# A projection by seven block products instead of eight, in two passes over halves of the tokens

## The chip, the cores and the metric

One Trainium2 chip, one core. The metric is device time in microseconds (us), the median of several runs of the whole program. The program is one layer of a decoder trunk; the change is in its first stage, the combined input projection.

## The reference

```python
h = rms_norm(x, g_mix[l])            # x: (1, 2048, 1024) float32
proj = h @ w_in[l]                   # w_in: 1024 x 7168
qkv = proj[..., :4608]               # q, k, v of three attention groups, 512 columns each
u = proj[..., 4608:5120]
gate_a, gate_b = proj[..., 5120:6144], proj[..., 6144:]
q = head_rms_norm(qkv[:, :, 0], q_gain[l]) * (HEAD_DIM ** -0.5)
k = head_rms_norm(qkv[:, :, 1], k_gain[l])
...                                  # attention, state space model, their mix, 32 experts
```

So the projection is a product of 2048 x 1024 by 1024 x 7168, with a sigmoid on the gates and a mean of squares over each head of 64 columns for q and k.

## The kernel before

`project` runs first (from 2.5 to 1283 us of the trace). Its 7168 columns are 14 matrices of 512 columns: u, then v, q and k of three groups, then four of gates. Each number is split into a high and a low part (fp32r), and a product is three matmuls: high by high, high by low, low by high.

All the tokens stay in SBUF, turned, as `hh` and `hl` (1024 x 2048 each). They are made in the first matrix, one token tile of 128 ahead: ScalarE squares (L520) and takes the root (L525), VectorE scales (L614), TensorE turns by eight transposes (L443), ScalarE writes the high part (L530) and VectorE the low one (L620).

For each matrix, 8 slices of the weights (128 x 512, `raw`) are loaded by SP's queue (L320) and split by ScalarE (`wh`, L542) and VectorE (`wl`, L625). Then 16 tiles of output follow, each of 8 slices x 3 = 24 matmuls of 128 x 128 by 128 x 512 into one of six PSUM banks (`po`, L493): 14 x 16 x 24 = 5376 matmuls. ScalarE takes u, v and gates out of PSUM (L561). A q or k tile takes five steps on two engines: squares on ScalarE (L551), a sum of each head (L634) and its mean (L637) on VectorE, roots on ScalarE (L553), and on VectorE the reciprocal (L639) and the product out of PSUM (L645). SP's queue stores each tile (L338).

The order on each engine is the order in which the code is written, tile by tile; one engine lets another go by semaphores. GpSimd makes 16 pairs of maps for the state space model beside the gate matrices (L274 to L303), and TensorE and VectorE finish a pair between two tiles (L456, L463, L787 to L794). VectorE computes the powers that these need in one piece (`maps`, beside a q matrix) and the tables in another (`table`).

## Time and profile before

| | |
|---|---|
| median of 3 runs | 4809.84 us (4809.36 to 4812.94) |
| the profiled execution | 4809.9 us, its span 4808.3 us |
| projection, first to last matmul of L493 | 15.9 to 1283 us |
| TensorE busy over the span | 97% |
| VectorE, ScalarE, GpSimd busy | 57%, 40%, 15% |
| granted TensorE clock | 0.987 of full speed (2.4 GHz) |

A matmul's duration in the profile (390 ns) is longer than the distance from one to the next, since they are pipelined: what counts is how many start in a stretch. The busy share of an engine is an average over stages that have different limits. A row of the timeline gives start, duration, engine, line, operation, and in brackets how long the engine had been idle and who ended that.

### The profile page before, as it was taken

What the parts mean: (1) busy time and instruction counts of PE and PEld (TensorE: products, weight loads), DVE (VectorE), ACT (ScalarE), POOL (GpSimd) and SP (SyncE); (2) the same over time, 40 slices, a digit from 0 to 9 for tenths busy, and PEclk for the clock granted to TensorE, in tenths of its full rate; (3) what the DMA queues carried; (4) which work ended last, traced back from release to release, by engine and by line L of the source; (5) the groups of instructions that cost most, each with busy time, mean ns of one, the idle gap of its engine ahead of it and who ended that gap; (6) DMA issues with size and microseconds to landing.
All of it is one profiled execution on the core that took longest, in us unless ns stands there. A gap on an engine that the chain in (4) does not pass through costs nothing.

```text
span 4808.3 us, 75561 instructions
## 1 busy us (share of the span) xinstructions
PE 4674.5 (97%) x26332; PEld 4097.3 (85%) x26332; DVE 2757.7 (57%) x5732; ACT 1916.0 (40%) x3152; POOL 697.2 (15%) x783
## 2 busy tenths in 40 slices
PE   8999999999889999999799999999999999999998
PEld 7888888878679987788699999999988888999997
DVE  4343333111266678555555556666667777778887
ACT  4212112111136673133233334344445555556665
POOL 0000000233202101222101111111111111111121
PEclk9999999999999999999899999999999999999999
DMA  4322222322453445543445555656566667677777
GB/s 136 115 71 77 73 85 81 115 90 91 128 205 136 139 163 184 185 134 136 176 151 176 189 177 190 204 179 215 179 229 215 208 231 241 237 244 268 279 262 254
DMA packets 262082, 823.24 MB, mean 171 GB/s; under 512 B 39273, under 2 KB 70804, under 8 KB 224341
## 3 DMA queue, kind: packets, MB, share of 16 engines
q1 hardware_dynamic: 228728, 715.02, 41.3%
q0 software_dynamic: 28304, 88.03, 7.9%
q10 hardware_dynamic: 4829, 17.31, 1.0%
q8 instruction: 131, 2.15, 0.2%
q14 instruction: 90, 0.74, 0.0%
HBM read 661.67 MB, written 163.88 MB: 172 GB/s over the span
## 4 chain that ended last, share of the span: by engine, by line
PE 51%; DVE 0%; ACT 0%; issue 0%; DVEq 0%; POOL 0%; DMA 0%; ACTq 0%; SPq 0%; POOLq 0%
PE ex_d L2453 14%; PE ex_g L2420 10%; PE ex_g L2422 9%; PE ex_g L2416 7%; PE ex_d L2416 4%; PE ex_d L2447 3%; PE ex_d L2422 2%; PE ex_g L2397 1%; PE ex_d L2397 0%; PE ex_d L2428 0%; DVEq L2224 0%; ACT ex_wgh L2500 0%; DVE ex_x L2615 0%; DVE ex_y L2689 0%; DVE ex_wgl L2597 0%
## 5 line engine op out<-in xcount | busy, mean ns | idle before, releaser
L2422 PE MATMUL ex_g<-ex_x,ex_wgl 128*128 128x256 f32 (+12 forms) x3456 | 980.0, 284 | 0.0
L2420 PE MATMUL ex_g<-ex_x,ex_wgh 128*128 128x288 f32 (+5 forms) x3584 | 756.1, 303 | 1.7 <-DVE ex_x L2615 1.7
L2422 PEld LDWEIGHTS ex_g<-ex_x,ex_wgl 128*128 128x128 f32 x3456 | 652.3, 189 | 4.3
L2597 DVE TENSOR_TENSOR ex_wgl<-ex_wg,ex_wgh 128x2048 fp32r<-128x2048 f32 x274 | 626.8, 2288 | 42.4 <-ACT ex_wgh L2500 42.3
L2500 ACT ACTIVATE ex_wgh<-ex_wg 128x2048 fp32r<-128x2048 f32 x274 | 523.5, 1910 | 280.7 <-PE ex_g L2422 274.0
L2420 PEld LDWEIGHTS ex_g<-ex_x,ex_wgh 128*128 128x128 f32 x3584 | 592.7, 188 | 11.1 <-DVE ex_x L2615 2.0
L2416 PE MATMUL ex_g<-ex_x,ex_wgh 128*128 128x512 f32 (+6 forms) x1664 | 527.5, 375 | 0.9 <-DVE ex_t L2627 0.9
L493 PE MATMUL prj_p<-prj_wh,prj_hh 128*128 128x512 f32 x1280 | 500.9, 391 | 1.4 <-DVE prj_hl L620 1.4
L493 PE MATMUL prj_p<-prj_wh,prj_hl 128*128 128x512 f32 x1280 | 499.0, 390 | 0.0
L493 PE MATMUL prj_p<-prj_wl,prj_hh 128*128 128x512 f32 x1280 | 499.0, 390 | 0.0
L2453 PE MATMUL ex_d<-ex_wdh,ex_ath 128*128 128x512 f32 x992 | 398.4, 402 | 1.1 <-DVE ex_ath L2655 1.1
L2453 PE MATMUL ex_d<-ex_wdh,ex_atl 128*128 128x512 f32 x992 | 391.1, 394 | 0.0
L2453 PE MATMUL ex_d<-ex_wdl,ex_ath 128*128 128x512 f32 x992 | 391.0, 394 | 0.0
L2365 POOL DMA_INDIRECT out<-ex_y,ex_cur x82 | 155.5, 1897 | 1513.4 <-ACT ex_y L2521 1246.6
L2507 ACT ACTIVATE ex_wdh<-ex_wd 128x1024 fp32r<-128x1024 f32 x273 | 287.8, 1054 | 180.1 <-PE ex_d L2447 116.8
L2416 PEld LDWEIGHTS ex_g<-ex_x,ex_wgh 128*128 128x128 f32 x1664 | 312.2, 188 | 42.6 <-issue 1.2
L2603 DVE TENSOR_TENSOR ex_wdl<-ex_wd,ex_wdh 128x1024 fp32r<-128x1024 f32 x272 | 331.8, 1220 | 21.5 <-ACT ex_wdh L2507 20.7
L493 PEld LDWEIGHTS prj_p<-prj_wh,prj_hh 128*128 128x128 f32 x1280 | 241.0, 188 | 52.0 <-DVE prj_hl L620 1.8
L2638 DVE TENSOR_SCALAR ex_t<-ex_g,ex_bgu 128x320 f32<-128x320 f32 (+5 forms) x112 | 60.2, 537 | 392.5 <-PE ex_g L2422 392.2
L561 ACT ACTIVATE prj_o<-prj_p 128x512 f32<-128x512 f32 x128 | 76.5, 598 | 520.1 <-PE prj_p L493 516.6
L493 PEld LDWEIGHTS prj_p<-prj_wh,prj_hl 128*128 128x128 f32 x1280 | 240.9, 188 | 50.3
L493 PEld LDWEIGHTS prj_p<-prj_wl,prj_hh 128*128 128x128 f32 x1280 | 241.1, 188 | 49.6
(429 smaller groups left out, 8775.8 us busy)
## 6 DMA issues: line engine op xcount, KB each, us to landing
ex_wg<-in_w_gu SPq DMA_DIRECT2D x276, 1024.0 KB, 5.2
ex_wd<-in_w_down SPq DMA_DIRECT2D x276, 512.0 KB, 6.6
qkv_d<-prj_o SPq DMA_DIRECT2D x144, 256.0 KB, 2.0
wo_spare<-qkv_d SPq DMA_DIRECT2D x40, 768.0 KB, 4.3
prj_raw<-in_w_in SPq DMA_DIRECT2D x109, 256.0 KB, 3.3
ex_bd<-in_b_down SPq DMA_DIRECT2D x34, 512.0 KB, 8.4
gate_d<-prj_o SPq DMA_DIRECT2D x64, 256.0 KB, 2.0
mix_ring<-gate_d SPq DMA_DIRECT2D x32, 512.0 KB, 4.3
```

The lines of the kernel that those rows point to most:

```text
L493: last = pe.matmul(po[n % OB][:, :], lhs, rhs, start=(k == 0 and j == 0), stop=(k == KD - 1 and j == 2))
L561: act.activation(ot[n % OR][:, :], po[n % OB][:, :], ACT.Sigmoid if kind == GATE else ACT.Copy).then_inc(o_ready, 1)
L2365: pool.indirect_dma_start(out=acc_d, out_offset=bass.IndirectOffsetOnAxis(ap=cur[:, g, 0:1].bitcast(U32), axis=0), in_=y[:, g, :], in_offs ...
L2416: pe.matmul(out[:, 0:2 * size].rearrange("p (r n) -> p r n", r=2), h[:, k, j, :], xs[:, :, k, 0:size], start=(k == 0), stop=False)
L2420: pe.matmul(out[:, 0:size], h[:, k, j, :], x[:, k, 0:size], start=(k == 0 and x is xh), stop=False)
L2422: last = pe.matmul(out[:, 0:size], l[:, k, j, :], xh[:, k, 0:size], start=False, stop=(k == KD - 1))
L2447: last = pe.matmul(out[0:m, :], ath[z][:, g * P:g * P + m], w[z][:, cols], start=(f == 0 and m == P), stop=(f == NF - 1 and m == P))
L2453: last = pe.matmul(out[:, :], a[z][:, g * P:(g + 1) * P], w[z][:, cols], start=(f == 0 and a is ath and w is wdh), stop=(f == NF - 1 and a ...
L2500: act.activation(flat(wgh[f % 2][:, :, :, :]), flat(wg[f % RAW][:, :, :, :]), ACT.Copy).then_inc(wgh_ready, 1)
L2507: act.activation(wdh[f % 2][:, :], wd[f % RAW][:, :], ACT.Copy).then_inc(wdh_ready, 1)
L2597: tt(flat(wgl[z][:, :, :, :]), flat(wg[r][:, :, :, :]), flat(wgh[z][:, :, :, :]).bitcast(F32), ALU.subtract).then_inc(wgl_ready, 1)
L2603: tt(wdl[z][:, :], wd[r][:, :], wdh[z][:, :].bitcast(F32), ALU.subtract).then_inc(wdl_ready, 1)
```

## The change

The matrices are taken in pairs of 1024 columns. Tokens are taken in two halves of 1024, weights in four blocks (upper and lower 512 rows, the two matrices). For a half, a pair is a 2 x 2 block product, which takes seven products of sums of blocks in place of eight (`seven`). One product is 4 steps of 12 matmuls, one step for each 128 tokens (or gate columns). The first pair in the first half is still done with eight (`plain`). The steps number 8 x 4 + 13 x 7 x 4 = 396, of 12 matmuls each: 4752.

- The weight sums are made by GpSimd, at 28 places 5 steps apart (`SUM_AT`): SP's queue loads four slices, GpSimd does four additions, and SP's queue stores four slices to DRAM (`sums_d`) three steps after. The second half reads the same sums.
- The sums of token blocks are made by GpSimd at 8 places (`PAIR_AT`): SP's queue loads two tiles of x, ScalarE and VectorE normalise them, GpSimd does four additions, SP's queue stores the results (`comb_d`). They are read again as 44 blocks of 128 x 512, each of them turned by four transposes (`turn_block`), and split.
- A weight slice is loaded and split once for each product: 99 x 4 = 396 slices in place of 112. There are 5 buffers for raw slices and 6 for split ones.
- Out of PSUM: products that others need go to SBUF (`ua`, `ub`) by ScalarE while the bank goes on accumulating; in three of seven products VectorE adds this to PSUM; a gate's sigmoid and a head's squares and scaling then work on the tile in SBUF.
- The maps and tables of VectorE are cut into pieces, five or two pieces a step. Of the numbers above, `g` is the step, `j` the step in its product.

```diff
-    XR, RAW, RING, OR, OB = 3, 4, 9, 3, 6
-    MAPS, TABLES, BIAS = 3, 6, 9
+    XR, RAW, RING, OR, KH = 3, 5, 6, 4, KD // 2
+    NJ, NQ = CH // P, 7
+    CONST, CONST_AT = 10, (3, 6, 9, 12)
+    BIAS = 9
...
+    mats = [(COPY, (QKV, None), qkv(0, 2)), (COPY, qkv(1, 2), qkv(2, 2)), (GATE, gate(0), gate(1)), (GATE, gate(2), gate(3))]
+    mats += [(Q, qkv(g, 0), qkv(g, 1)) for g in range(NG)]
+
...
+    seven = [(A11, ("w", 0, 0), True, "c1"), (A12, ("w", 1, 0), True, "c11"), (S2, ("t", T2), False, "u2"),
+             (S3, ("t", T3), False, "u3"), (A22, ("t", T4), False, "all"), (S1, ("t", T1), True, "c22"),
+             (S4, ("w", 1, 1), False, "c12")]
...
+    prods = []
+    for half, order in ((0, (0, 1, 2, 3, 4, 5, 6)), (1, (0, 1, 4, 5, 6, 2, 3))):
+        for q in order:
+            direct = (half, q) == (0, 0)
+            for (o, b, start, post), to in zip(plain if direct else seven, plain_to if direct else seven_to):
+                prods.append((half, q, o, b, start, post, to))
...
+    TILE_AT = {1: 2, 2: 3, 9: 4, 11: 5, 13: 6, 15: 7}
+    PAIR_AT = (16, 21, 26, 31, 60, 66, 72, 78)
+    SUM_AT = [8 + 5 * k for k in range(NQ * KH)]
+    SUMS = [(q, kk) for q in (1, 2, 3, 4, 5, 6, 0) for kk in range(KH)]
...
+                def weight_sums(k):
+                    b11, b12, b21, b22 = wt
+                    pool.wait_ge(sum_in, 64 * k + 64)
+                    go_sum(pool.tensor_tensor(b11[:, :], b12[:, :], b11[:, :], ALU.subtract))
+                    pool.tensor_tensor(b12[:, :], b22[:, :], b12[:, :], ALU.subtract).then_inc(sum_ready, 1)
...
+                for g in range(SUM_AT[-1] + 1):
+                    if g in SUM_AT:
+                        weight_sums(SUM_AT.index(g))
+                    if g - 2 in PAIR_AT:
+                        row_sums(PAIR_AT.index(g - 2))
...
+                def load_pair(n):
...
+                    sp.wait_ge(comb_out, stored[n])
+                    load_x(2 * NJ + 2 * n)
+                    load_x(2 * NJ + 2 * n + 1)
...
+                def store_row_sums(n):
+                    xl, xu, z = xt
+                    lo, hi = slice(0, AW), slice(AW, D)
+                    for i, (o, src) in enumerate(((S1, z[:, lo]), (S3, z[:, hi]), (S2, xu[:, lo]), (S4, xl[:, hi]))):
+                        sp.wait_ge(comb_ready, 4 * n + i + 1)
+                        sp.dma_start(comb_d[n, o], src).then_inc(comb_out, 16)
+                    if n >= NJ:
+                        sp.wait_ge(a12_out, 16 * (n - NJ + 1))
+                        sp.sem_inc(comb_out, 16)
+
+                def load_sums(k):
+                    q, kk = SUMS[k]
+                    if k:
+                        sp.wait_ge(sum_out, 64 * k)
+                    for n, (upper, which) in enumerate(((0, 0), (0, 1), (1, 0), (1, 1))):
+                        r, col = upper * KH + kk, mats[q][1 + which][0]
+                        sp.dma_start(wt[n][:, :], w_in[r * P:(r + 1) * P, col:col + AW]).then_inc(sum_in, 16)
+
+                def store_sums(k):
+                    q, kk = SUMS[k]
+                    sp.wait_ge(sum_ready, 2 * k + 2)
+                    for n in range(4):
+                        sp.dma_start(sums_d[q, n, kk], wt[n][:, :]).then_inc(sum_out, 16)
...
+                for g in range(NSTEP):
...
+                    while left and store_at(left[0]) <= g:
+                        store(left.pop(0))
+                    ahead = min(NS, (g // NJ + 1) * KH + RAW + (0, 0, 1, 2)[g % NJ])
+                    while loaded < ahead:
                         load_slice(loaded)
                         loaded += 1
+                    if g - 5 in PAIR_AT:
+                        store_row_sums(PAIR_AT.index(g - 5))
+                    if g - 4 in PAIR_AT:
+                        store_rows_of(PAIR_AT.index(g - 4))
+                    if g in PAIR_AT:
+                        load_pair(PAIR_AT.index(g))
+                    if g - 3 in SUM_AT:
+                        store_sums(SUM_AT.index(g - 3))
+                    if g in SUM_AT:
+                        load_sums(SUM_AT.index(g))
...
+                def turn_block(i):
+                    src, sem, value = block_buf(i)
+                    pe.wait_ge(sem, value)
+                    pe.wait_ge(low_ready, i - 1)
+                    for k in range(4):
+                        last = pe.transpose(pt[i % 2][:, k * P:(k + 1) * P], src[:, k * P:(k + 1) * P], ident[:, :])
+                    last.then_inc(turned, 1)
...
+                    if g in needs:
+                        pe.wait_ge(low_ready, needs[g])
+                    if bank_free[g]:
+                        who, value = bank_free[g]
+                        pe.wait_ge(act_done if who == "act" else dve_done, value)
...
+                def gate_out(g):
+                    if g in out_of and out_of[g] in g_no:
+                        e = out_of[g]
+                        act.wait_ge(dve_done, dve_post[g])
+                        act.activation(ot[e % OR][:, :], ot[e % OR][:, :], ACT.Sigmoid).then_inc(gated, 1)
+
...
+                    tt(ot[e % OR][:, :], bank(g)[:, :], u_of(g)[:, :], ALU.add).then_inc(dve_done, 1)
+
+                def head_means(g):
+                    if g in out_of and out_of[g] in q_no:
+                        i = q_no[out_of[g]]
+                        dve.wait_ge(sq_ready, i + 1)
...
+                def head_scales(g):
+                    if g in out_of and out_of[g] in q_no:
+                        e = out_of[g]
+                        i = q_no[e]
+                        dve.wait_ge(hrms_ready, i + 1)
+                        dve.reciprocal(hrstd[:, i % 2, :], hrms[:, i % 2, :]).then_inc(hrstd_ready, 1)
+                        dve.wait_ge(hrstd_ready, i + 1)
+                        heads = ot[e % OR][:, :].rearrange("p (h d) -> p h d", h=HG)
+                        tt(heads, heads, hrstd[:, i % 2, :].unsqueeze(2).to_broadcast([P, HG, DH]),
+                           ALU.mult).then_inc(q_done, 1)
...
+                    head_scales(g - 3)
+                    head_means(g - 2)
+                    if g:
+                        leave(g - 1)
+                    if g < NSTEP:
+                        for s in splits_at(g):
                             split(s)
+                    if g in block_at:
+                        low(block_at[g])
+                    if g - 2 in PAIR_AT:
+                        n = 2 * NJ + 2 * PAIR_AT.index(g - 2)
+                        for i in (n, n + 1):
+                            mean(i)
+                            normalise(i)
+                    if g - 1 in pair_at:
+                        save_pair(pair_at[g - 1])
+                    if MAPS <= g < TABLES:
+                        some(making_maps, 5)
+                    if g >= TABLES:
+                        some(making_tables, 2)
...
```

SP's queue, in the first pair of matrices, before: an output stored (`u_d`), a tile of x loaded, now and then a slice of weights, each waiting for one event.

```order
L338 DMA u_d<-prj_o 128x512 [waits prj_o_ready]
L320 DMA prj_raw<-in_w_in 128x512 [waits prj_wl_ready]
L325 DMA prj_x<-in_x 128x1024 [waits prj_turned]
L338 DMA u_d<-prj_o 128x512 [waits prj_o_ready]
L325 DMA prj_x<-in_x 128x1024 [waits prj_turned]
```

The same queue now, around step 31. `prj_wt` are the four slices of a weight sum, `comb_d` and `sums_d` the sums in DRAM.

```order
L451 DMA prj_raw<-in_w_in 128x512 [waits prj_wl_ready]
L487 DMA comb_d<-prj_x 128x512 [waits prj_comb_ready] x4
L461 DMA prj_x<-in_x 128x1024 [waits prj_comb_out]
L461 DMA prj_x<-in_x 128x1024
L504 DMA sums_d<-prj_wt 128x512 [waits prj_sum_ready]
L504 DMA sums_d<-prj_wt 128x512 x3
L451 DMA prj_raw<-in_w_in 128x512 [waits prj_wl_ready] x3
L498 DMA prj_wt<-in_w_in 128x512 [waits prj_sum_out]
L498 DMA prj_wt<-in_w_in 128x512 x3
```

Between two loads of weight slices for TensorE stand waits for GpSimd (`comb_ready`, `sum_ready`) and for stores that must have landed (`comb_out`, `sum_out`).

VectorE in a q or k matrix, before: one tile, and the next begins with the same rows.

```order
L634 TENSOR_REDUCE prj_hss<-prj_sq 128x8
L637 TENSOR_SCALAR prj_hms<-prj_hss 128x8
L639 RECIPROCAL prj_hrstd<-prj_hrms 128x8
L645 TENSOR_TENSOR prj_o<-prj_p,prj_hrstd 128x512
L625 TENSOR_TENSOR prj_wl<-prj_raw,prj_wh 128x512
```

VectorE in a q and k pair now, from the last step of a product whose tile it adds (`ua`) into the next (`ub`).

```order
L901 TENSOR_SCALAR prj_hms<-prj_hss 128x8 [waits prj_hss_ready]
L892 TENSOR_TENSOR prj_o<-prj_p,prj_ua 128x512 [waits prj_o_out3,prj_act_done,prj_mm]
L908 RECIPROCAL prj_hrstd<-prj_hrms 128x8 [waits prj_hrms_ready]
L911 TENSOR_TENSOR prj_o<-prj_o,prj_hrstd 128x512 [waits prj_hrstd_ready]
L898 TENSOR_REDUCE prj_hss<-prj_sq 128x8 [waits prj_sq_ready]
L901 TENSOR_SCALAR prj_hms<-prj_hss 128x8 [waits prj_hss_ready]
L892 TENSOR_TENSOR prj_o<-prj_p,prj_ub 128x512 [waits prj_o_out0,prj_act_done,prj_mm]
L881 TENSOR_TENSOR prj_wl<-prj_raw,prj_wh 128x512 [waits prj_wh_ready]
```

The scaling (L911) now reads SBUF twice where L645 read PSUM, an addition (L892) and a split (L881) have come in, and this stands in a step of 12 matmuls where it stood in one of 24.

## Rows read from the trace of the kernel before

**Rows 1.** The page: busy time of the engines, and a group of the projection's matmuls.

```profile
PE 4674.5 (97%) x26332; PEld 4097.3 (85%) x26332; DVE 2757.7 (57%) x5732; ACT 1916.0 (40%) x3152; POOL 697.2 (15%) x783
L493 PE MATMUL prj_p<-prj_wh,prj_hh 128*128 128x512 f32 x1280 | 500.9, 391 | 1.4 <-DVE prj_hl L620 1.4
```

**Rows 2.** Windows, all engines: stretch, length, busy us (and count) of PE, PEld, DVE, ACT, POOL.

```profile
300.00:850.00 550.00, 550.00 (x2428) 455.59 (x2427) 205.98 (x713) 104.87 (x220) 0.00 (x0) 1.00 0.23 78
```

**Rows 3.** Waits of TensorE from 15 to 1290 us: us in total, times, longest.

```profile
PE prj_t L443 <- DVE prj_x L614: 2.1, 1, 2.1
```

**Rows 4.** Timeline, TensorE: a tile turned between matmuls, and one after an idle gap.

```profile
20.46 1.04 PE L443 MATMUL prj_t<-k_ident,prj_x 128*128 128x128 f32 x8
21.25 0.47 PE L493 MATMUL prj_p<-prj_wh,prj_hh 128*128 128x512 f32 x1
...
26.41 1.97 PE L443 MATMUL prj_t<-k_ident,prj_x 128*128 128x128 f32 x8 [2.15 <-DVE prj_x L614]
28.02 0.77 PE L493 MATMUL prj_p<-prj_wh,prj_hh 128*128 128x512 f32 x1
...
29.85 0.40 PE L493 MATMUL prj_p<-prj_wl,prj_hh 128*128 128x512 f32 x1
```

**Rows 5.** DMA issues to 2100 us: KB each, median us from issue to landing.

```profile
prj_raw<-in_w_in SPq DMA_DIRECT2D x109, 256.0 KB, 3.3
qkv_d<-prj_o SPq DMA_DIRECT2D x144, 256.0 KB, 2.0
yT_d<-s_yT SPq DMA_DIRECT2D x4, 1024.0 KB, 4.2
```

**Rows 6.** Timeline, SP's queue: two loads issued one after another, and a store.

```profile
2.92 0.90 SPq L320 DMA_DIRECT2D prj_raw<-in_w_in  x2
...
29.52 0.33 SPq L338 DMA_DIRECT2D u_d<-prj_o  x1
```

**Rows 7.** One line, GpSimd: an addition of 128 x 512 (duration ns min/median/max).

```profile
L1791 POOL TENSOR_TENSOR sp_rows<-sp_rows,mix_tb x32: 1262/1300/1610, 1830.9 to 2035.4; 128x512 f32<-128x512 f32 x32
```

**Rows 8.** Timeline: VectorE, then GpSimd, where a split met a map.

```profile
1125.78 1.22 DVE L625 TENSOR_TENSOR prj_wl<-prj_raw,prj_wh 128x512 fp32r<-128x512 f32 x1 [5.44 <-ACT prj_wh L542]
...
1125.67 0.78 POOL L289 TENSOR_TENSOR prj_x<-prj_x 128x272 f32<-128x272 f32 x1
1126.53 0.95 POOL L274 TENSOR_TENSOR prj_gb<-prj_rr,prj_br 128x256 f32<-128x256 f32 x1
1127.44 0.61 POOL L274 TENSOR_TENSOR prj_gb<-prj_ri,prj_bi 128x256 f32<-128x256 f32 x1
```

**Rows 9.** Groups by line to 1283 us, VectorE: busy us, mean ns, idle before.

```profile
L625 DVE TENSOR_TENSOR prj_wl<-prj_raw,prj_wh 128x512 fp32r<-128x512 f32 x109 | 73.9, 697 | 213.1 <-ACT prj_wh L542 212.3
...
L634 DVE TENSOR_REDUCE prj_hss<-prj_sq 128x8 f32<-128x512 f32 x96 | 65.8, 685 | 287.4 <-ACT prj_sq L551 287.3
...
L639 DVE RECIPROCAL prj_hrstd<-prj_hrms 128x8 f32<-128x8 f32 x96 | 19.5, 203 | 26.8 <-ACT prj_hrms L553 26.8
L637 DVE TENSOR_SCALAR prj_hms<-prj_hss 128x8 f32<-128x8 f32 x96 | 16.5, 172 | 3.3
```

**Rows 10.** Timeline, ScalarE: one tile squared and rooted.

```profile
29.38 0.63 ACT L520 ACTIVATE prj_sq<-prj_x 128x512 f32<-128x512 f32 x1
...
31.27 0.20 ACT L525 ACTIVATE prj_rms<-prj_ms 128x1 f32<-128x1 f32 x1 [0.41 <-DVE prj_ms L605]
```

**Rows 11.** Timeline, VectorE: a split runs on from a scaling; a pair's part begins and ends.

```profile
500.09 0.69 DVE L645 TENSOR_TENSOR prj_o<-prj_p,prj_hrstd 128x512 f32<-128x512 f32 x1
500.70 0.68 DVE L625 TENSOR_TENSOR prj_wl<-prj_raw,prj_wh 128x512 fp32r<-128x512 f32 x1
...
966.67 0.69 DVE L787 COPY prj_gb<-prj_t 128x512 f32<-128x512 f32 x1 [11.82 <-PE prj_t L456]
...
968.85 0.17 DVE L779 TENSOR_SCALAR prj_x<-prj_bi 64x16 f32<-64x16 f32 x1
```

**Rows 12.** Groups by line to 1283 us, ScalarE: the load of a function table.

```profile
L525 ACT ACT_TABLE_LOAD x1 | 1.3, 1283 | 0.0
```

More of the change, by code:

```diff
@@ L797, in save_pair, with tables, some @@
                         blocks(p + 2)
+                def tables():
+                    for b in range(PAIRS // BP):
+                        yield from table(b)
+                def some(work, n):
+                    for _ in range(n):
+                        if next(work, None) is None:
+                            return
                 mean(0)
```

689 lines of the change are left out of this document (430 added, 259 removed).

## The prediction

> **What bounds the kernel now.** I read the page first: TensorE is busy 97% of the span, and a group of the projection's matmuls alone costs 501 us, 391 ns each [rows 1]. Those 391 ns overlap the next matmul, so I count starts: from 300 to 850 us TensorE is busy throughout, at full clock, and starts 2428 matmuls, 0.2265 us each [rows 2]. The waits of TensorE from its first matmul to the projection's end are 2.1 us for a scaled tile [rows 3] and 1.4 us for the first low part [rows 1]. So this stage is bound by TensorE and nothing else, and matmuls that are left out are gained as long as whatever feeds it keeps up. In the same 550 us VectorE works 206 us and ScalarE 105 us [rows 2]: there is room, but the change puts most of its new work there and on two parts that have been idle, GpSimd and SP's queue. The question is which of these chains becomes longer than the matmuls beside it.
>
> **What is removed.** 5376 matmuls become 4752: 624 less, 624 x 0.2265 = 141.3 us. One step of 12 now takes 2.72 us, five steps 13.6 us.
>
> **What TensorE gets in addition.** 240 transposes in place of 128. Eight of them start at 20.46 and the next matmul at 21.25 us, where it would have started at 20.46 [rows 4], 0.1 us each: 112 x 0.1 = 11 us. The first four tiles are wanted one a step, 2.7 us apart, where they were wanted one in 5.4 us; a tile goes through square, root, scaling, transposes and split one after the other, 2.1 us on ScalarE alone [rows 10]. That leaves TensorE about one step behind at the start: 3 us.
>
> **The chain of a weight sum.** Four loads of 256 KB are issued 0.45 us apart [rows 6] and one lands after 3.3 us [rows 5]: 4 x 0.45 + 3.3 = 5.1 us. Four additions on GpSimd at 1.30 us [rows 7]: 5.2 us. Four stores, issued 0.33 us apart [rows 6], land 2.0 us after issue [rows 5], so 3.0 us, or 4.2 us if they go like one store of 1 MB [rows 5]; I take 3.6. Handing on costs 0.3 us. Sum 14.2 us, and the next sum's loads wait for the last store. The code gives a sum 13.6 us. SP's queue stands in both waits, and behind it stand the slices that TensorE needs.
>
> To this comes contention. A split on VectorE that began while GpSimd was in an addition took 1.22 us in place of 0.70, and GpSimd's next one 0.95 in place of 0.61 [rows 8]: each waits for the other's whole instruction. A step has one split, so two fall into the four additions, some 0.5 us each: 15.2 us a sum, 1.6 us over its five steps. After the last pair of token tiles 12 such sums remain: 19 us, of which I take off 4, since part of them lie in q and k steps that are slow anyway: **15 us**. The bounds are 0 (sum of 13.6 us or less) and 12 x 3.4 = 41 us (17 us, if each addition took GpSimd's longest 1.61 us and splits came on top [rows 7]).
>
> The Trainium skill (GPSIMD Engine Reference, section 8, Key points) says that GpSimd contends for its SBUF interfaces with VectorE instructions that have two SBUF inputs. The trace agrees where a split reads raw and high part. By it the scaling of q and k, which now reads its tile from SBUF, joins them, and that is how I cost it below.
>
> **The pairs of token tiles.** At steps 16, 21, 26 and 31 a pair is added to the same queues. SP's queue waits for the four row sums, GpSimd makes them only after the weight sum in front, the next pair's load waits until they are stored, and the weight sum's stores are issued after that. One round: loads 5.1, weight sum 5.2, row sums 5.2, last store 0.33 + 2.0, two loads of x issued 0.9 (as two loads of [rows 6]), stores 3.6, handing on 0.4: 22.7 us, and with 1.3 us of contention 24. Against 13.6 that is 10.4 us too long, four times 42. Off it go what SP's queue is ahead (slices are loaded one to five steps early, some 5 us) and the last round, which has no further pair (3 us): **34 us**. It shows twice over: ScalarE stands in the square of a pair whose x is late, in front of the splits of the next product. The bounds are 15 us (ahead by a whole product, 10.9 us, and stores that overlap) and 45 us.
>
> The second four pairs are 6 steps apart, 16.3 us, but sums stay 5 apart. From step 60 to 83 are 62.6 us; the same parts laid end to end come to about 85. Of the 22 us I take 7 off for slices loaded ahead, and add 3 for contention: **18 us**, bounds 5 and 26.
>
> Each stop of TensorE costs clock besides. After 2.15 us of idling the eight transposes took 1.6 us to the next matmul in place of 0.8, and the four matmuls after it started 0.43 us apart, 29.85 being the first at the full distance again [rows 4]: 1.6 us a stop. Four stops: **6 us** (0 to 12).
>
> **VectorE in q and k pairs.** A step with an addition costs the split 0.63 (one operation of this size follows another after 0.61 us [rows 11]), the addition 0.63, the reduction and its mean 0.86, the reciprocal 0.20 [rows 9] and the scaling 0.63: 2.95 us against 2.72. Eight such steps follow one another (products `c22` and `c12`), which puts VectorE 1.8 us behind, and 1 us of that is covered by slices already split. While GpSimd works, two operations of each step can meet it; at half its time that is 0.65 us in the first pair (weight sums), 0.45 us in the second half (maps). So 6 us for the first pair, 4.5 for each of two in the second half, 1 to 2 us for the three others: **20 us** of six pairs. Bounds 5 and 47 us: if in all six pairs each of the 12 steps with an addition is late by 0.65 us, 47 us. Beside that the state space pairs: VectorE's part of one takes 2.3 us [rows 11], TensorE's hardly more than 1; half of the 16 now fall into q and k steps: **5 us** (0 to 10). `maps` is cut into pieces of 2 us a step beside 1 us of other work, and ten more function tables are loaded at 1.28 us [rows 12], most with room around them: **4 us** (0 to 10). 284 more splits and 44 more blocks are hidden elsewhere: a product that gives nothing out costs VectorE and ScalarE one split a step, under 1 us of 2.72.
>
> **The sum.** -141.3 + 11 + 3 + 15 + 34 + 18 + 6 + 20 + 5 + 4 = -25 us. The profiled execution took 4809.9 us (its span and 1.6 us), the median is 4809.84: no difference to carry. 4810 - 25 = 4785 us.
>
> **The rivals.**
> 1. *SP's queue stays ahead.* The weight sum takes 13.6 us or less and the slices loaded early cover most of each round. For it: loads and stores of different buffers overlap in the queues, and the DMA engines are 23% busy [rows 2]. Against it: the waits are in one queue and no round can begin before the last is stored. Time: -141.3 + 14 of TensorE's own + 15 + 5 of the pairs + 3 of clock + 12 of VectorE + 0 + 4 = -88: **4722 us**.
> 2. *GpSimd decides, and the kernel is slower.* If additions and splits shut each other out more often than one in two, a sum takes 17 us. Then the sums cost 41, the pairs 45 + 26, the clock 12, VectorE's q and k passes 38, state space pairs and maps 12: 174, less 141.3 - 14 = 127: 47 us slower, **4857 us**. It becomes slower from the point where the losses pass 127 us, that is with additions at 1.55 us in place of 1.30. For it: every one of the 396 splits reads SBUF twice. Against it: the mean of 109 splits is 0.70 us [rows 9], beside GpSimd's maps too.
> 3. *Only VectorE changes hands.* The sums keep up half way, but the chain of additions, squares, roots and scalings over three engines makes each q and k pass 8 us late in place of 3: 5 x 6 = 30 us more than in the sum, **4812 us**, no difference to be seen.
> 4. *It does not do what it says*: the number of matmuls is fixed by the code, so this only could fail by records; I give it nothing.
>
> **How the numbers follow.** The forecast (4755 to 4800) gets 0.42, the first rival (4700 to 4755) 0.20, the third 0.14, the second 0.24. What can be told from no change is 0.2%, 9.6 us, so the same is 4800 to 4819. Faster: 0.42 + 0.20 and a little of the third, 0.63; same 0.12; slower 0.25. The range that leaves out 2 in 10 goes from 4715 to 4850: the first rival's centre at one end, most of the second at the other.
>
> **What would show it.** The projection's 4752 matmuls would end near 1258 us. In the waits of TensorE the largest should be at steps 27 to 39 and about 76: first matmuls of products waiting for the low part of a slice (VectorE), behind it ScalarE waiting for x, behind that SP's queue waiting for GpSimd. GpSimd's four additions should take 5.2 us or more, and a sum 15 us from load to load. The low clock should stand in the slices from 100 to 300 us. If SP's queue shows no waits for GpSimd above 3 us, rival 1 holds; if additions average over 1.55 us, rival 2; if TensorE's waits lie between steps 116 and 200 and behind 256, rival 3. I would be wrong altogether if the time changed after the projection, where I expect nothing.

## The result and the profile after

The changed kernel takes 4882.34 us (4881.65 to 4885.10, 5 runs), the kernel before in the same session 4810.97 us: a ratio of 1.0150, 95% interval 1.0139 to 1.0162. It is 71 us slower where 25 us less were forecast, and lies outside the range.

All of it arises in the projection. Its last matmul, on the timeline of TensorE, before and after:

```profile
1282.61 0.39 PE L493 MATMUL prj_p<-prj_hh,prj_wl 128*128 128x512 f32 x1
```

```profile
1351.99 0.39 PE L713 MATMUL prj_p<-prj_ah,prj_wl 128*128 128x512 f32 x1
```

That is 69.4 us later; from there to the end of the profiled span it is 3526 us before and 3528 us after. From here on this moment is the measure, the **end** for short: kernels that leave sums out change the data, and with it the work after the projection.

The page, as in [rows 1]: TensorE's share of busy time is three points lower, GpSimd's four points higher, and a split on VectorE takes 801 ns where [rows 9] has 697.

```profile
PE 4600.5 (94%) x25820; PEld 4013.6 (82%) x25820; DVE 3137.4 (64%) x6232; ACT 2197.6 (45%) x3658; POOL 943.4 (19%) x927
L881 DVE TENSOR_TENSOR prj_wl<-prj_raw,prj_wh 128x512 fp32r<-128x512 f32 x396 | 312.5, 801 | 312.9 <-ACT prj_wh L766 312.2
```

The waits of TensorE from 15 to 1400 us (total, times, longest), which answer to [rows 3]:

```profile
PE prj_p L713 <- DVE prj_wl L881: 105.2, 30, 20.2
PE prj_t L662 <- DMA prj_x<-comb_d: 13.5, 5, 11.5
PE prj_t L653 <- DVE prj_x L870: 10.4, 7, 2.9
...
PE prj_p L713 <- ACT prj_o L776: 8.5, 1, 8.5
```

Where they lie, in windows with the columns of [rows 2]; the last three are the granted clock, the busy share of the DMA engines and GB/s:

```profile
96.00:205.00 109.00, 61.92 (x228) 48.58 (x226) 30.40 (x49) 26.81 (x62) 44.14 (x33) 0.78 0.64 218
205.00:600.00 395.00, 320.37 (x1297) 251.32 (x1298) 212.73 (x481) 152.45 (x280) 141.79 (x101) 0.90 0.76 263
620.00:900.00 280.00, 280.00 (x1290) 231.70 (x1289) 182.63 (x453) 128.96 (x249) 0.00 (x0) 1.00 0.58 181
900.00:1200.00 300.00, 287.52 (x1238) 228.21 (x1237) 205.04 (x421) 124.11 (x248) 101.36 (x120) 0.98 0.52 168
```

At 0.2265 us a matmul, 109 us hold 481 and 395 us hold 1744. Of the instructions counted, 6 and 60 are transposes (0.1 us each [rows 4]), 222 and 1237 matmuls of the product: 259 and 507 are missing, about 58 and 109 us. From 620 us on, when the last sum is stored, TensorE never stops until the maps of the state space begin. So the loss is the stretch of the sums. VectorE works only 213 of the 395 us there, and whether its 801 ns a split matter all the same is left to the experiments.

One round of a pair shows why. SP's queue first, then GpSimd, ScalarE and TensorE, each on its timeline:

```profile
119.86 1.76 SPq L498 DMA_DIRECT2D prj_wt<-in_w_in  x4
...
133.27 4.29 SPq L487 DMA_DIRECT2D comb_d<-prj_x  x4
139.24 0.81 SPq L461 DMA_DIRECT2D prj_x<-in_x  x2
140.09 2.50 SPq L504 DMA_DIRECT2D sums_d<-prj_wt  x4
142.63 2.73 SPq L451 DMA_DIRECT2D prj_raw<-in_w_in  x3
148.12 1.75 SPq L498 DMA_DIRECT2D prj_wt<-in_w_in  x4
```

```profile
126.34 1.27 POOL L369 TENSOR_TENSOR prj_wt<-prj_wt 128x512 f32<-128x512 f32 x1 [17.77 <-DMA prj_wt<-in_w_in]
...
130.73 1.28 POOL L372 TENSOR_TENSOR prj_wt<-prj_wt 128x512 f32<-128x512 f32 x1
131.97 1.27 POOL L378 TENSOR_TENSOR prj_x<-prj_x 128x512 f32<-128x512 f32 x1
...
154.88 1.30 POOL L369 TENSOR_TENSOR prj_wt<-prj_wt 128x512 f32<-128x512 f32 x1 [17.68 <-DMA prj_wt<-in_w_in]
```

```profile
143.60 0.63 ACT L743 ACTIVATE prj_sq<-prj_x 128x512 f32<-128x512 f32 x1 [15.36 <-DMA prj_x<-in_x]
```

```profile
149.96 0.77 PE L713 MATMUL prj_p<-prj_wh,prj_ah 128*128 128x512 f32 x1 [9.66 <-DVE prj_wl L881]
```

SP's queue issues weight blocks at 119.86, cannot go on past the row sums until GpSimd has made them (133.27), loads x at 139.24, stores weight sums at 140.09 and only then loads the next slices (142.63) and the next weight blocks (148.12): 28.3 us from load to load, for five steps that take 13.6 us together. ScalarE stands 15.4 us before that x, with splits queued behind it, and TensorE stands at the end. Outside the pairs the same chain without row sums takes 17.2 us from the first addition of one sum to that of the next (nine sums from 455.3 to 609.7 us on the timeline). The waits of SP's queue from 15 to 640 us, the three largest for another engine's sums or stores:

```profile
SPq L504 <- POOL prj_wt L372: 122.0, 19, 9.5
...
SPq L487 <- POOL prj_x L378: 46.1, 5, 10.4
SPq L498 <- DMA sums_d<-prj_wt: 24.1, 16, 3.7
```

### The profile page after: what moved, and what is told of

Its sections match the earlier page's. It is cut to its first block, busy times and chain, and to the rows that moved or that the text cites. A ratio compares the mean times of both kernels' runs of the same rounds, so it can differ in the third digit from the quotient of the medians.

```text
span 4879.8 us, 77081 instructions
## 1 busy us (share of the span) xinstructions
PE 4600.5 (94%) x25820; PEld 4013.6 (82%) x25820; DVE 3137.4 (64%) x6232; ACT 2197.6 (45%) x3658; POOL 943.4 (19%) x927
## 4 chain that ended last, share of the span: by engine, by line
PE 50%; DVE 0%; ACT 0%; issue 0%; DVEq 0%; POOL 0%; DMA 0%; ACTq 0%; SPq 0%; POOLq 0%
PE ex_d L2771 14%; PE ex_g L2738 10%; PE ex_g L2740 9%; PE ex_g L2734 7%; PE ex_d L2734 4%; PE ex_d L2765 3%; PE ex_d L2740 2%; PE ex_g L2715 1%; PE ex_d L2715 0%; PE ex_d L2746 0%; DVEq L2542 0%; ACT ex_wgh L2818 0%; DVE ex_x L2933 0%; DVE ex_y L3007 0%; DVE ex_wgl L2915 0%
## 5 line engine op out<-in xcount | busy, mean ns | idle before, releaser
L713 PE MATMUL prj_p<-prj_wh,prj_ah 128*128 128x512 f32 x1136 | 462.6, 407 | 68.9 <-DVE prj_wl L881 54.8
L881 DVE TENSOR_TENSOR prj_wl<-prj_raw,prj_wh 128x512 fp32r<-128x512 f32 x396 | 312.5, 801 | 312.9 <-ACT prj_wh L766 312.2
L713 PE MATMUL prj_p<-prj_wl,prj_ah 128*128 128x512 f32 x1136 | 453.2, 399 | 0.0
L713 PE MATMUL prj_p<-prj_wh,prj_al 128*128 128x512 f32 x1136 | 452.8, 399 | 0.0
L713 PEld LDWEIGHTS prj_p<-prj_wh,prj_ah 128*128 128x128 f32 x1136 | 220.2, 194 | 127.1 <-DVE prj_wl L881 53.0
L766 ACT ACTIVATE prj_wh<-prj_raw 128x512 fp32r<-128x512 f32 x396 | 244.9, 626 | 161.3 <-PE prj_p L713 120.8
L713 PEld LDWEIGHTS prj_p<-prj_wh,prj_al 128*128 128x128 f32 x1136 | 219.7, 193 | 48.3
```

Of the source, the lines that this page charges most:

```text
L713: last = pe.matmul(bank(g)[:, :], lhs, rhs, start=(start and kk == 0 and n == 0), stop=(kk == KH - 1 and n == 2), skip_group_check=True)
L766: act.activation(wh[:, s % RING, :], raw[s % RAW][:, :], ACT.Copy).then_inc(wh_ready, 1)
L881: tt(wl[:, s % RING, :], raw[s % RAW][:, :], wh[:, s % RING, :].bitcast(F32), ALU.subtract).then_inc(wl_ready, 1)
```

## The experiments

Each kernel was timed beside the kernel before on the same chip; the chips of different rows can differ. Where sums are left out, or their additions cut to one column, only the end is comparable:

| kernel | end, us | kernel, us |
|---|---|---|
| before | 1282.6 | 4811 |
| changed | 1352.0 | 4882 |
| `e1`: no weight sums | 1226.2 | - |
| `e2`: no row sums | 1281.0 | - |
| `e3`: neither | 1188.3 | - |
| `e4`: additions of one column | 1259.6 | - |
| `e5`: two sets of buffers for weight sums | 1333.8 | 4866 |
| `e6`: before, with additions nobody needs | 1282.1 | 4813 |
| `e7`: `e5` and the second four pairs apart | 1294.6 | 4828 |
| `e8`: `e7`, all pairs apart, two pairs of matrices plain | 1242.9 | 4777 |
| `e9`: `e2` with two sets | 1225.2 | - |
| `e10`: `e8` with a weight sum every six steps | 1249.4 | 4786 |
| `e11`: `e8` with one set | 1334.9 | 4867 |
| `e12`: `e8` with additions of one column | 1228.5 | - |

An end is that of the one execution that was profiled. Executions of one kernel differ by up to 10 us (`e11`: 4859.9 to 4870.0), so differences below that tell little.

### Without weight sums, without row sums, without both

`e1`: T slices come straight from the weights, no set is loaded, added or stored.

```diff
-                    if g in SUM_AT:
-                        weight_sums(SUM_AT.index(g))
...
-                        src = sums_d[q, b[1], kk]
+                        src = w_in[kk * P:(kk + 1) * P, col:col + AW]
```

> Left out: all 28 weight sums with their loads, additions and stores; the T slices are read from the weight matrix itself, so the output differs, and the time is read at the end of the projection's matmuls (changed kernel: about 1358 us; before: 1283 us). Theory (a serial round trip: load into the one set of four buffers, add, store, wait for the store to land, load again, all through SyncE's one queue, takes 17.1 us where five steps take 13.6): from 205 to 600 us the changed kernel made 105 steps, 285 us of matmuls at full rate, in 395 us, so about 110 us go, and some of the waits in the first four pairs' rounds; the end lies at 1200 to 1250 us. Rival 'the row-sum pairs do it' : less than 50 us go and the end stays above 1300 us. Rival 'half-rate clock and the extra work on VectorE and ScalarE everywhere': the same, above 1300 us.

Measured: end 1226.2 us, 125.8 us before the changed kernel's 1352.0 (the expectation counts from 1358), within what the theory gave; both rivals fall.

`e2`: no pair is loaded, normalised, added or stored.

```diff
-                    if g in PAIR_AT:
-                        load_pair(PAIR_AT.index(g))
...
-                    sp.dma_start(dst, comb_d[NJ * half + j, o]).then_inc(sem, 16)
+                    sp.dma_start(dst, x[t * P:(t + 1) * P, at_:at_ + AW]).then_inc(sem, 16)
```

> Left out: the eight pairs' loads, normalisation, row sums and stores; the S blocks and the second pass's blocks are read straight from the input, so the output differs; read at the begin of the projection's last matmul (changed kernel 1352.0 us, without weight sums 1226.2). Theory A (the weight sums' serial round trip of 17.1 us paces everything up to step 146): the 28 round trips alone take 28 x 17.1 = 479 us from 55 us on, so the sums end at about 535 us instead of 620 and the last matmul begins at 1265 to 1290 us. Theory B (what costs is that pairs and weight sums share SyncE's queue and GpSimd: a pair's round that holds a weight sum takes 28 us, one alone some 18): without the pairs nearly all goes, the end lies at 1210 to 1240 us.

Measured: end 1281.0 us, as theory A had it; theory B falls. The weight sums alone, with nothing beside them, run from 54.5 to 537.7 us (the first of the four additions: its line in GpSimd's instructions, with min/median/max in ns and first and last start):

```profile
L369 POOL TENSOR_TENSOR prj_wt<-prj_wt x28: 1260/1288/1809, 54.5 to 537.7; 128x512 f32<-128x512 f32 x28
```

483.2 / 27 = 17.9 us a sum, for the 13.6 us of five steps.

`e3`: both edits together.

> Left out: the weight sums and the row sums both, with all their transfers; the seven products, their 4752 matmuls and their combination by ScalarE and VectorE stay. The output differs. Read at the begin of the last matmul: it bounds what any arrangement of the sums can give. Both theories: the stalls before 620 us go altogether; the kernel without weight sums was still short of some 145 matmuls of the full rate between 100 and 350 us (33 us) and of a few before, so the end lies at 1175 to 1200 us. Were it above 1215 us, the combination work on VectorE and ScalarE would cost 30 us or more by itself.

Measured: end 1188.3 us, in the range. In its windows TensorE stops for 1.9 of 500 us before the state space (2109 of the 2267 are matmuls of the product, 156 transposes), and for 11.6 of 300 us beside its maps:

```profile
100.00:600.00 500.00, 498.11 (x2267) 411.12 (x2266) 286.57 (x704) 237.44 (x438) 0.95 (x1) 1.00 0.56 175
800.00:1100.00 300.00, 288.42 (x1243) 228.34 (x1242) 205.64 (x420) 126.29 (x248) 137.68 (x168) 0.98 0.54 170
```

These three take the loss apart. Seven products without any sums end 94.3 us before the kernel before. The row sums alone cost 1226.2 - 1188.3 = 37.9 us, the weight sums alone 1281.0 - 1188.3 = 92.7 us, both together 163.7: **33 us** more than their sum. The constants of the state space are computed within the first of the two windows, five pieces a step as in the changed kernel, and cost nothing there.

### GpSimd's additions by themselves

`e4`: each addition of the changed kernel on one column, everything else kept.

```diff
-                    go_sum(pool.tensor_tensor(b11[:, :], b12[:, :], b11[:, :], ALU.subtract))
+                    go_sum(pool.tensor_tensor(b11[:, 0:1], b12[:, 0:1], b11[:, 0:1], ALU.subtract))
```

> Every load, store and wait of the changed kernel is kept, but each GpSimd addition of the weight sums and row sums works on one column instead of 512, so the output differs; read at the end of the projection (changed kernel 1358 us). Theory (serial round trip): the 5.7 us of additions leave a round trip of 17.1, which becomes about 11.5 us and fits under the 13.6 us of five steps outside the pairs; in the pairs' rounds 5.5 us of 28 go. End at 1210 to 1270 us. Rival 'the transfers themselves are too slow under load, the additions are beside the point': the end stays above 1320 us. Rival 'GpSimd and VectorE hold each other up': as the theory, but then a split on VectorE goes back from 801 ns to about 700 and the gain stays away where the additions are kept and only the serial wait is removed (the kernel with two sets).

Measured: end 1259.6 us, 92 us earlier, as the theory gave it. A split takes 728 ns in place of 801. Shorter additions shorten the round trip and free VectorE; that alone doesn't tell the chain from contention. `e6` measures contention by itself, and `e5` and `e9` mend the chain with every addition kept.

`e6`: the kernel before, with additions that nobody needs.

```diff
+                for k in range(40):
+                    pool.wait_ge(o_ready, 17 + 2 * k)
+                    for n in range(5):
+                        pool.wait_ge(idle_set, 5 * k + n + 1)
+                        pool.tensor_tensor(idle[0][:, :], idle[0][:, :], idle[0][:, :], ALU.add).then_inc(idle_set, 1)
```

> The kernel before with GpSimd additions that nobody needs: 200 additions of 384 columns in 40 groups, one group every second unit of 5.4 us from unit 17 to 95 of the projection, and no transfers with them. It measures by itself what GpSimd's additions do to VectorE and TensorE. Theory (serial round trip): VectorE's splits beside them go from 697 ns to about 800, but with nothing waiting on GpSimd the kernel stays within 10 us of 4811. Rival 'GpSimd and VectorE hold each other up, and that paces TensorE': GpSimd is busy for some 250 us, more than the 205 us of the changed kernel's additions, so the kernel is 50 us or more longer.

Measured: 4812.66 us, ratio 1.0005 (0.9995 to 1.0014), end 1282.1 us. Its window over the additions, and VectorE's splits in the same stretch, in the kernel before (L625) and in this one (L633):

```profile
90.00:520.00 430.00, 429.80 (x1909) 354.97 (x1908) 197.18 (x526) 93.24 (x202) 158.99 (x182) 1.00 0.24 84
```

```profile
L625 DVE TENSOR_TENSOR prj_wl<-prj_raw,prj_wh 128x512 fp32r<-128x512 f32 x40 | 26.6, 688 | 51.1 <-ACT prj_wh L542 50.7
L633 DVE TENSOR_TENSOR prj_wl<-prj_raw,prj_wh 128x512 fp32r<-128x512 f32 x40 | 37.9, 982 | 31.4 <-ACT prj_wh L550 31.2
```

GpSimd works 159 of 430 us (five additions of 384 columns in a row, 876 ns each), a split takes 982 ns where the kernel before has 688 in that stretch (the theory gave 800), and TensorE stops for 0.2 us in all. Contention is real and costs nothing so long as nobody waits for either engine. This kernel has one split in 10.8 us where the changed one has one in a step of 2.7, so it doesn't show that contention is free there.

### A second set of buffers

`e5`: eight buffers for weight sums; a set is stored 8 steps after its load, and its next load waits for a store two steps old. The memory is that of the state-space constants, whose computation moves from step 92 to 160.

```diff
         wt = [t_.sb(f"wt{n}", [P, AW]) for n in range(4)]
+        late = t_.sb("late", [P, sum(PAIRS * w for _, w in prm)])
+        wt += [late[:, n * AW:(n + 1) * AW] for n in range(4)]
...
-                    if g - 3 in SUM_AT:
-                        store_sums(SUM_AT.index(g - 3))
+                    if g - 8 in SUM_AT:
+                        store_sums(SUM_AT.index(g - 8))
```

> A second set of four buffers for the weight sums (in the memory of the state-space constants, whose computation is moved from step 92 to step 160 for it); a set is loaded every 5 steps as before, stored 8 steps after its load instead of 3, and its next load waits for a store issued 2 steps earlier. Every addition and every transfer is kept, the output is the reference's. Theory (serial round trip): SyncE no longer waits for the sums; the loss of about 110 us from 205 to 600 us goes nearly whole, the pairs' waits stay. End of the projection 1230 to 1270 us (changed kernel 1358), kernel 4755 to 4800 us (changed 4882, before 4811). Rival 'GpSimd and VectorE hold each other up': the additions are all there, so the end stays at 1330 to 1358 us and the kernel above 4850 us. Rival 'transfers too slow under load': the same, since the bytes are the same.

Measured: 4865.9 us (ratio to before 1.0112, 1.0095 to 1.0128), end 1333.8 us: 18 us gained where the theory gave 80 to 120. Taken by the number, the rivals win. The windows say otherwise:

```profile
100.00:200.00 100.00, 54.26 (x205) 42.74 (x203) 25.48 (x44) 25.05 (x58) 43.18 (x32) 0.80 0.60 211
400.00:600.00 200.00, 194.76 (x837) 158.31 (x837) 118.95 (x178) 88.76 (x166) 71.73 (x48) 0.99 0.87 294
600.00:700.00 100.00, 83.14 (x346) 65.65 (x345) 86.16 (x351) 44.14 (x86) 0.00 (x0) 0.90 0.46 144
```

From 400 to 600 us the changed kernel has 654 instructions of TensorE and this one 837: 41 us gained, where for the most part weight sums stand alone. (The constants left this stretch too, but they cost nothing in `e3`.) From 600 to 700 us it has 346 against 437, of which 32 and 8 are transposes, some 23 us lost: the constants' pieces, five a step, now meet a q and k pass, and VectorE is busy 86%. And from 100 to 200 us next to nothing changed (205 against 197): there the pairs' rounds decide, whatever the buffers. So the theory of one chain was too simple: there are two in turn, and the mended one is hidden behind the other for half of the way. The 18 us are what is left of a larger gain after the constants' new place is paid for.

`e9`: the kernel without row sums, with the second set, so that only weight sums are left. The constants start at step 160 here too, three pieces a step.

> The kernel without row sums, with the second set of four buffers for the weight sums (stored 8 steps after their load, the constants' computation at step 160). The output differs, the row sums are left out; read at the begin of the projection's last matmul: 1281.0 us without row sums with one set, 1188.3 without either kind of sum. Theory (one set of buffers makes load, additions and stores a serial round trip, measured there at 17.9 us per sum for the 13.6 us of five steps): of the 93 us that the weight sums cost when they are alone nearly all go, the last matmul begins at 1195 to 1215 us. Rival (the weight sums cost by their bytes and by GpSimd's time, whatever the buffers; in the whole kernel the second set gave 18 us only): 1245 us or later.

Measured: end 1225.2 us, 55.8 us earlier than with one set, between the ranges of the theory (10 us later) and of the rival (20 us earlier). What is left over the kernel with neither is 37 us, in part at 500 to 600 us, where TensorE stops for 10.8 us and the moved constants again meet VectorE; the rest wasn't traced:

```profile
500.00:600.00 100.00, 89.22 (x397) 71.33 (x396) 86.52 (x339) 49.12 (x96) 0.00 (x0) 0.97 0.50 160
```

### The pairs apart

`e7`: on top of `e5`, the second four pairs 14 steps apart, stored 10 steps after their load, and the constants two pieces a step.

```diff
-    PAIR_AT = (16, 21, 26, 31, 60, 66, 72, 78)
+    PAIR_AT = (16, 21, 26, 31, 60, 74, 88, 102)
```

> The kernel with two sets, and in it the second four pairs are loaded at steps 60, 74, 88 and 102 instead of 60, 66, 72 and 78, their normalisation 3 steps and their stores 10 steps after the load; the state-space constants are computed with 2 pieces a step instead of 5, from step 158. The output is the reference's. Theory (a pair's load has to wait in SyncE's queue for the stores of the pair before, and ScalarE waits in its own queue for that load, so that splits behind it are late): with 14 steps (38 us) per pair nothing waits; between 300 and 400 us the kernel with two sets made 269 matmuls where 443 is the full rate, 39 us, and between 600 and 700 us 346, 22 us. Both go: the last matmul begins at about 1270 to 1285 us instead of 1333.8, the kernel takes 4800 to 4820 us. Rival (the transfers are at their limit, 305 to 328 GB/s between 200 and 500 us): spreading the same bytes moves the loss along, the end stays above 1315 us.

Measured: 4828.2 us (1.0038, 1.0023 to 1.0052), end 1294.6 us: 39 us gained, 10 us short of the theory's range and 20 us under the rival's. From 300 to 400 us it has 407 instructions against 268, 31 us, the pairs' part, and from 600 to 700 us 363 of the product's matmuls against 313, the part of the slower constants. How the 39 us divide between the two edits wasn't run.

`e8`: besides, the second pair of matrices of the first pass in eight products, so that row sums are wanted 32 steps later and the first four pairs can be 11 steps apart, the second four 12.

```diff
-            direct = (half, q) == (0, 0)
+            direct = half == 0 and q < 2
...
+    PAIR_AT = (16, 27, 38, 49, 92, 104, 116, 128)
```

> As the kernel with the second pairs apart, and the second pair of matrices of the first pass is also done in eight products (48 matmuls more, 11 us), so that the first row sums are needed 32 steps later; the pairs are loaded at steps 16, 27, 38, 49 and 92, 104, 116, 128, normalised 3 and stored 9 steps after. The output is the reference's. Theory: between 100 and 200 us the kernel with two sets made 205 matmuls where 443 is the full rate, 53 us; they go, for 11 us of matmuls: the last matmul begins at 1225 to 1250 us, and the kernel takes 4755 to 4785 us, faster than before (4811). Rival (transfers at their limit, or GpSimd's own time of 5.7 us per weight sum and of a pair's additions): at least half of that stays, the end above 1270 us.

Measured: 4776.9 us, ratio 0.9931 (0.9915 to 0.9948), end 1242.9 us, as the theory gave it. From 100 to 200 us, as above for `e5`:

```profile
100.00:200.00 100.00, 95.11 (x414) 76.69 (x412) 55.04 (x60) 39.65 (x84) 64.78 (x44) 1.00 0.96 341
```

414 in place of 205, 47 us, with GpSimd busier than in `e5` (65 us against 43). This kernel is 0.7% faster than the kernel before.

`e11`: `e8` with one set of buffers, stored after 3 steps.

> The kernel with two plain pairs of matrices and the pairs of row blocks apart, but with one set of four buffers for the weight sums, stored 3 steps after their load, as in the changed kernel. The output is the reference's. Theory (the serial round trip of one set costs by itself, the pairs' rounds by themselves, and 33 us more come from both together): the pairs' rounds stay mended, the sums' round trip of 17 to 18 us is back: 28 of them take about 490 us instead of 380, the last matmul begins at 1300 to 1330 us and the kernel takes 4835 to 4865 us. Rival (only the pairs' rounds mattered, as the 18 us of the second set in the whole kernel suggest): the last matmul within 20 us of 1243, the kernel below 4800 us.

Measured: 4867.5 us (1.0109, 1.0092 to 1.0126), end 1334.9 us: 92 us lost, 5 and 2 us beyond the theory's ranges. With the pairs apart, the second set and the later store are worth 92 us; beside the pairs close together they were worth 18, net of the constants. The pairs apart with one set (`e11`) end only 17 us before the changed kernel, and both mendings (`e8`) 109 us before it. Each mending alone shows a fraction of its worth, because the other chain takes over.

### What holds the best one

`e10`: `e8` with a weight sum every 6 steps; the constants start at step 184, three pieces a step.

```diff
-    SUM_AT = [8 + 5 * k for k in range(NQ * KH)]
+    SUM_AT = [8 + 6 * k for k in range(NQ * KH)]
```

> The kernel with two plain pairs of matrices, and its weight sums loaded every 6 steps instead of every 5 (the constants' computation then starts at step 184). The output is the reference's. That kernel moved 332 to 349 GB/s between 300 and 500 us, with the DMA engines 94 to 98% busy, and made 784 matmuls there where 886 is the full rate, 23 us short; its last matmul began at 1242.9 us, some 44 us above what the kernel without sums would give with its 48 more matmuls. Theory (with the waits gone, the transfers are the limit there): a sixth less traffic of the sums, so 10 to 25 us go: last matmul at 1218 to 1233 us, kernel 4752 to 4767 us (4777 for every 5). Rival (the loss is in the queues' order and in VectorE's work): within 5 us of 1243 and of 4777.

Measured: 4786.1 us (0.9948, 0.9931 to 0.9964), end 1249.4 us: not earlier, and a little later than either range. From 300 to 500 us, `e8` and then this one:

```profile
300.00:500.00 200.00, 182.07 (x782) 147.15 (x781) 115.82 (x158) 98.86 (x188) 98.82 (x65) 0.97 0.96 344
```

```profile
300.00:500.00 200.00, 183.32 (x779) 147.86 (x778) 112.72 (x151) 97.84 (x185) 86.51 (x60) 0.97 0.90 323
```

The transfers fall from 344 to 323 GB/s and TensorE does the same work: the rate of transfer wasn't the limit there.

`e12`: `e8` with additions of one column.

> The kernel with two plain pairs of matrices, every load, store and wait kept, but each GpSimd addition of the weight sums and row sums works on one column, so the output differs; read at the begin of the projection's last matmul (1242.9 us with the whole additions; some 1199 us would be left without any sums). It splits the 44 us that remain. Theory C (GpSimd and VectorE hold each other up: from 60 to 470 us the splits there took 1092 ns on average and the additions 1446 to 1612 ns): splits go back to about 700 ns, and half or more of the 44 us goes; the last matmul at 1205 to 1222 us. Theory L (transfers at 343 to 349 GB/s and the order in SyncE's queue): at most 10 us go, 1233 us or later.

Measured: end 1228.5 us, 14 of the 44 us, between the two theories' ranges. Splits are back at 690 ns (1092 in `e8`, from 60 to 470 us), yet 30 us stay. From 100 to 200 us TensorE is busy all but 0.5 us beside the highest transfer rate that any run has in such a window of its projection:

```profile
100.00:200.00 100.00, 99.47 (x439) 82.07 (x438) 34.31 (x60) 40.09 (x84) 11.89 (x40) 1.00 0.98 354
```

Where those 30 us lie I can name only in part: between 300 and 500 us 801 of 883 are made (19 us). VectorE's combinations wait for output buffers whose stores to `gate_d` haven't landed (21 us of VectorE's idle time from 60 to 470 us); that TensorE's stops come from these waits is not shown, and a further output buffer wasn't tried.

## Why the prediction was wrong

**Bound of the kernel before:** right. 4752 matmuls and all that comes with the seven products but the sums: the prediction has -141.3 + 11 + 3 + 20 + 5 + 4 = -98 us, the kernel with neither sum has -94.3. The total fits better than its parts. By 800 us that kernel has started 3245 of the product's matmuls and the kernel before 3373, 29 us, and after it falls back by another 18 us. The prediction has 18 us for transposes, first tiles and constants, and 25 us for VectorE in q and k passes and for the state space pairs.

**VectorE in q and k passes, 20 us:** near in size, wrong in place. The q and k passes of the first half cost nothing after the sums (TensorE doesn't stop from 620 to 900 us). The loss lies in the second half, where q and k passes, state space pairs and GpSimd's maps meet: from 900 to 1200 us the changed kernel starts 1166 of the product's matmuls and the kernel before, beside the same maps, 1236: 16 us. Which of the three makes it wasn't separated.

**The chain of a weight sum, 15 us (0 to 41):** the step that failed most; alone it costs 93 us. Two things in it. First, the length: 17.9 us in place of 15.2. A round of the kernel without row sums (`e2`), on the timelines of SP's queue and GpSimd:

```profile
205.81 1.79 SPq L502 DMA_DIRECT2D sums_d<-prj_wt  x4
211.06 2.45 SPq L496 DMA_DIRECT2D prj_wt<-in_w_in  x4
218.73 1.29 POOL L369 TENSOR_TENSOR prj_wt<-prj_wt 128x512 f32<-128x512 f32 x1 [12.94 <-DMA prj_wt<-in_w_in]
225.27 2.05 SPq L502 DMA_DIRECT2D sums_d<-prj_wt  x4
```

This one takes 19.5 us, and the 27 rounds 17.9 us on average. Stores until the next load take 4.9 us of it (3.6 in the sum), loads until the addition 6.8 (5.1), additions until the next stores 6.2, handing on included (6.2 and 0.3). So issuing and landing under load were short by 3 us, and GpSimd by nothing: [rows 5] gave 3.3 us for a landing in a kernel whose DMA engines are 23% busy [rows 2], where they are 74% busy here from 60 to 540 us. The page after has, with KB each and median us to landing:

```profile
prj_wt<-in_w_in SPq DMA_DIRECT2D x112, 256.0 KB, 4.3
sums_d<-prj_wt SPq DMA_DIRECT2D x112, 256.0 KB, 2.7
```

Second, the count: the prediction lets "12 such sums remain" after the pairs, and the five between the two groups of pairs (steps 38 to 58) are in no term. A chain that is too long for its five steps is too long for all 28, and 28 x (17.9 - 13.6) = 120 us is the bound, of which 93 were lost. The prediction had the excess of 1.6 us as the small difference of two large numbers, and then multiplied it by less than half of its places; the range should have carried 28 x 3.4 us. Its upper 17 us a sum isn't added up either: 14.2 us, four additions at 1.61 and 1 us of contention make 16.4.

**The pairs, 34 + 18 us:** alone they cost 38 us, with the weight sums in their rounds the two together cost 164, that is 71 for the pairs; 33 of them come only from both kinds of sum in one queue. The mechanism is as told, with SP's queue waiting for the four sums (POOL L378 ends 46.1 us of its waits) and ScalarE in the square of a late x (15.4 us); VectorE stands behind it in the pair's mean (L857, 81.2 us in 15 waits from 15 to 640 us). The size is not: the round shown takes 28.3 us in place of 24, and TensorE stopped for 8.5, 9.7, 14.2 and 11.5 us in the four rounds, where little was left of the 5 us that slices loaded ahead were to cover.

**Clock, 6 us (0 to 12):** too small. In the windows from 96 to 600 us TensorE is busy 382 us for 1459 matmuls and 66 transposes, which at 0.2265 and 0.1 us are 337: 45 us more. A part is the last matmul before each stop, which counts with its whole 0.4 us; the rest are matmuls at a granted clock of 0.78 and 0.90 on average. How it divides wasn't measured. They stand within the costs above, not beside them. The 1.6 us a stop were read nearly right: the four matmuls from 28.02 to 29.85 are 0.46 us apart on average, not 0.43.

**The rivals.** The second came nearest, 4857 us, and its figure of 17 us a sum was right. Its cause wasn't: additions average 1.33 to 1.49 us on the four lines, under its mark of 1.55. With every addition kept, two sets gave 56 us where weight sums are alone (`e9`), and all additions cut to one column gave 14 us once the chains were mended (`e12`). The prediction saw that a sum might take 17 us, but tied it to GpSimd's additions alone and gave it 0.24; the same 17 us through the landing of four transfers had no chance of its own. What the Trainium skill (GPSIMD Engine Reference, section 8, Key points) says, that GpSimd contends with VectorE instructions that have two SBUF inputs, holds in the durations of the split, which has two (982 ns beside additions, 688 without). It doesn't decide the time. The third rival's time is misadded: 30 us more than the sum are 4815 us, not 4812.

**What would show it:** the marks were good. The five largest stops of TensorE are where they were named (steps 27, 32, 36 and 39, and 20.2 us at step 76), behind the same three queues. The granted clock is 0.77 from 100 to 200 us, 0.95, 0.83 and 0.91 in the next three windows. The sum of 15 us from load to load was the mark that failed, and it was the term: from step 84 to 140 TensorE stops eleven times for 2 to 6 us, where nothing was named.

## What to carry to other kernels

A round trip through one buffer and one in-order queue (load, compute, store, wait, load) has to be shorter than the work beside it by a margin that covers transfers under load, and its excess counts as often as it runs; a second buffer and a store issued late turn it into throughput. Where two such chains share queues, mend both before judging either: here a second set with a late store was worth 18 us beside the close pairs (net of what the moved constants cost) and 92 us after they were set apart. Work that isn't urgent (constants, second-pass row sums) goes where the engine has idle time, not where the code first allows it.

## What the runs showed of the hardware

- GpSimd at 159 of 430 us beside VectorE lengthens each split from 688 to 982 ns and costs the kernel nothing; in the best kernel splits took 1092 ns on average between 60 and 470 us, and all of GpSimd's additions together were worth 14 us. In that kernel and stretch VectorE's instructions with two SBUF inputs are longer than with additions of one column: splits 1092 against 690 ns, scalings 725 against 692. Those that read one operand from PSUM (687 and 691) and reductions of one input (680 and 681) are not.
- Transfers at 354 GB/s, with the DMA engines busy 98%, didn't slow TensorE (439 instructions in 100 us, busy 99.5 us, at full clock). What grows is latency: a set of four 256 KB loads took 5.4 to 8.4 us from issue to the first addition, 6.8 on average (`e2`), and a store of 256 KB landed after 2.7 us in the changed kernel and 4.7 in `e8`, where [rows 5] has 2.0. SP's queue issued four stores in 1.8 us in most rounds of the changed kernel, and in 2.4 to 2.5 us in the four from 83 to 169 us (0.6 us each), where [rows 6] has 0.33 for one.
